# Two-block sequence kernel, fp32 on one core: reordering the second block's projections and the level steps of its gated linear attention

## The reference, cut to what matters

```
n = rms_norm(x, attn_norm_g)
proj = n @ w_in          # g_qkv (q 512, k 512, v 1024), g_lr 16, g_out 1024,
                         # nq 1024, kc vc ks vs kw vw 256 each, ng 24
g_qkv = silu(causal_short_conv(g_qkv, gla_conv_w))      # 4 taps along the tokens
log_a = log_sigmoid(g_lr @ gate_w2 + gate_b) / 16
# gated linear attention, chunks of 64 tokens, b = cumsum(log_a) in the chunk
scores = einsum('bhtd,bhsd,bhtsd->bhts', q, k, exp(b_t - b_s)), causal
o = scores @ v + (q * exp(b)) @ state;  state = decayed state + k^T v
gla_out = rms_norm(o) * silu(g_out)
nsa_out = compressed + selected + windowed attention over nq, kc, vc, ks, vs, kw, vw
h = x + concat([gla_out, nsa_out]) @ w_out
h + (silu(m @ w_gate) * (m @ w_up)) @ w_down            # m = rms_norm(h)
```

## Time and profile before

| | |
|---|---|
| median of 3 runs | 2771.13 us (2763.72 to 2773.09) |
| the profiled execution, its own time | 2766.11 us |
| its span, first to last instruction | 2764.1 us |
| granted TensorE clock, mean | 0.994 |
| TensorE busy | 2696.9 us, 98% of the span |
| VectorE, ScalarE, GpSimd busy | 1135.6, 1229.2, 1183.0 us (41%, 44%, 43%) |
| DMA | 489.00 MB, mean 177 GB/s |

### The profile page before, as it was taken

One profiled execution on the slowest core, in us unless ns is written; L12 is line 12 of the kernel. 1 busy time (PEld: TensorE's weight loads), 2 busy tenths in 40 slices (PEclk: granted clock), 3 DMA queues, 4 the chain that ended last, 5 costly groups with the idle time before them and its releaser, 6 DMA issues.

```text
span 2764.1 us, 33945 instructions
## 1 busy us (share of the span) xinstructions
PE 2696.9 (98%) x13886; PEld 2298.6 (83%) x13886; DVE 1135.6 (41%) x1363; ACT 1229.2 (44%) x1502; POOL 1183.0 (43%) x536
## 2 busy tenths in 40 slices
PE   9999999999999999999999978999999999999999
PEld 8998777778888888888888877988788888888887
DVE  6777654433432222232323477346432222232222
ACT  6434445444444444444444445535454444444333
POOL 3555553344444444444444334332244444444443
PEclk9999999999999999999999989999999999999999
DMA  6444445355555555555555532453355555555554
GB/s 235 163 158 155 156 139 174 137 198 187 193 183 189 192 186 195 185 192 191 196 192 198 180 129 101 170 189 124 132 184 185 193 187 191 190 188 193 197 199 152
DMA packets 73161, 489.00 MB, mean 177 GB/s; under 512 B 8443, under 2 KB 10140, under 8 KB 15536
## 3 DMA queue, kind: packets, MB, share of 16 engines
q1 hardware_dynamic: 73008, 486.84, 50.3%
HBM read 484.71 MB, written 2.10 MB: 176 GB/s over the span
## 4 chain that ended last, share of the span: by engine, by line
PE 85%; DVE 8%; ACT 3%; issue 3%; POOL 1%; DMA 1%; SPq 0%; DVEq 0%; ACTq 0%; POOLq 0%
PE PB L575 24%; PE PB L579 24%; PE PB L576 24%; PE PB L543 2%; PE PB L547 2%; PE PB L544 2%; ACT WH L1108 2%; PE PB L593 1%; DVE TM L2344 1%; DVE WL L1631 1%; DMA RAW<-in_w_in_a 1%; DVE TM L2341 1%; DVE TM L1683 1%; DVE TM L1674 1%; DVE TM L1686 0%
## 5 line engine op out<-in xcount | busy, mean ns | idle before, releaser
L2434 POOL TENSOR_TENSOR WL<-RAW,WH 128x1024 fp32r<-128x1024 f32 x442 | 1077.5, 2438 | 1462.4 <-ACT WH L1108 1462.4
L1108 ACT ACTIVATE WH<-RAW 128x1024 fp32r<-128x1024 f32 x892 | 939.6, 1058 | 1162.4 <-PE PB L579 1101.5
L1631 DVE TENSOR_TENSOR WL<-RAW,WH 128x1024 fp32r<-128x1024 f32 x450 | 581.8, 1294 | 1474.7 <-ACT WH L1108 1474.4
L575 PE MATMUL PB<-WH,HNH 128*128 128x512 f32 x1888 | 740.6, 392 | 5.0 <-DVE MIX L2279 4.6
L579 PE MATMUL PB<-WL,HNH 128*128 128x512 f32 x1888 | 735.5, 390 | 4.2 <-POOL WL L2434 4.2
L576 PE MATMUL PB<-WH,HNL 128*128 128x512 f32 x1888 | 735.1, 389 | 0.0
L575 PEld LDWEIGHTS PB<-WH,HNH 128*128 128x128 f32 x1888 | 354.6, 188 | 82.2 <-DVE MIX L2279 5.8
L579 PEld LDWEIGHTS PB<-WL,HNH 128*128 128x128 f32 x1888 | 354.6, 188 | 78.6 <-POOL WL L2434 4.6
L576 PEld LDWEIGHTS PB<-WH,HNL 128*128 128x128 f32 x1888 | 354.7, 188 | 72.1
L543 PE MATMUL PB<-HNH,WH 128*128 128x256 f32 x1184 | 347.1, 293 | 2.6 <-ACT WH L1108 2.4
L547 PE MATMUL PB<-HNH,WL 128*128 128x256 f32 x1184 | 339.4, 287 | 10.4 <-POOL WL L2434 6.0
(11 more groups left out here) (346 smaller groups left out, 2080.9 us busy)
## 6 DMA issues: line engine op xcount, KB each, us to landing
RAW<-in_w_gu SPq DMA_DIRECT2D x176, 1024.0 KB, 4.8
RAW<-in_w_dn SPq DMA_DIRECT2D x88, 1024.0 KB, 4.8
RAW<-in_w_in_a SPq DMA_DIRECT2D x56, 1024.0 KB, 4.8
RAW<-in_w_in SPq DMA_DIRECT2D x45, 1024.0 KB, 4.8
RAW<-in_w_out SPq DMA_DIRECT2D x32, 1024.0 KB, 4.8
RAW<-in_w_ga SPq DMA_DIRECT2D x24, 1024.0 KB, 4.8
RAW<-in_w_gb SPq DMA_DIRECT2D x24, 1024.0 KB, 4.8
WIN<-in_win SPq DMA_DIRECT2D x8, 512.0 KB, 5.8
```

Of the source, the lines that this page charges most:

```text
L575: e.matmul(o, hi[:, k, x], WH[:, s, c], start=k == 0, stop=False)
L1108: e.activation(WH[:, u % NSPL, :], RAW[:, n % NRAW, half * SU * 128:(half + 1) * SU * 128], ACT.Copy).then_inc(*wt.act.mark(("wh", u)))
L1631: e.tensor_tensor(WL[:, u % NSPL, :], RAW[:, n % NRAW, half * SU * 128:(half + 1) * SU * 128], f32(WH[:, u % NSPL, :]), ALU.subtract).then ...
L2434: e.tensor_tensor(WL[:, u % NSPL, :], RAW[:, n % NRAW, half * SU * 128:(half + 1) * SU * 128], f32(WH[:, u % NSPL, :]), ALU.subtract).then ...
```

## The change

- **Order of the projections.** `SECOND` becomes `og`, `ks`, `kc`, `v`, `vs`, `cmp`, `nq`, `mg`, and the weights are packed in that order. The number of tiles is the same.
- **Levels.** They run beside `og` and the first rows of `ks`. A fourth buffer of exponents is added (`GE3`, in memory that the queries `NQA` use later). VectorE's `before(lv)` and GpSimd's `after(lv)` stand in step 3 + lv, ScalarE's exponential in step 4 + lv, `keys(lv)` and `queries(lv)` in step 5 + lv, TensorE's matmuls in step 6 + lv, `taken(lv)` in step 7 + lv.
- **Convolutions.** VectorE now scales row j and does not convolve it there: `conv_next(j)` runs the three last taps of row j - 1 (`conv4`) and then scales row j. The first tap moves to ScalarE (`conv_first`, an activation with a scale, in the place of the `tensor_scalar`). The silus move one row back. The turning of `v` moves one tile back (tile 9 of the row).
- **Outputs.** The output part of the linear attention (`outputs`) starts eight quick steps into `vs` and ends in `cmp`; the norms of the keys and `CB` (`keys`) come ahead of it, beside `kc` and the first row of `v`. `CB` and a small norm buffer (`NB2`) move in memory.

The core of the diff (the moved helper functions of the other attention are unchanged and left out):

```diff
-        GE = [ar("GE0", [128, 4, T], 32), ar("GE1", [128, 4, T], 36), GG]
+        GE = [ar("GE0", [128, 4, T], 32), ar("GE1", [128, 4, T], 36), GG, ar("GE3", [128, 4, T], 76)]
...
-        CB = ar("CB", [128, 2, 32, 2, 15], 16)
+        CB = ar("CB", [128, 2, 32, 2, 15], 32)
...
-        SECOND = (("v", 8, 16), ("og", 2, 64), ("ks", 4, 16), ("kc", 4, 16), ("vs", 1, 64),
+        SECOND = (("og", 2, 64), ("ks", 4, 16), ("kc", 4, 16), ("v", 8, 16), ("vs", 1, 64),
...
+        def second(w, levels, keys, outputs, heads):
+
+            yield from levels
+            w.rate = 3.4 / 16.0
             yield from passed(w, "ks", 3)
-            for _ in range(4):
-                yield
+            yield from keys
+            w.passed.add("cb")
+            yield from passed(w, "v", 7)
+            yield from idle(8)
+            yield from outputs
+            yield from passed(w, "cmp", 1)
+            yield from heads
+
+        def other_levels():
+            return idle(14)
+
+        def other_keys(w):
+            yield from idle(4)
...
+        def other_outputs():
+            return idle(10)
...
-                        group(nt, HNH, HNL, 16)
+                        group(nt, HNH, HNL, 16, None, {1: values_turned})
                     elif name == "og":
-                        group(NT["og"] + 2 * j, HNH, HNL, 16, None, {} if j else {1: values_turned, 2: gates_turned})
+                        group(NT["og"] + 2 * j, HNH, HNL, 16, None, {} if j else {2: gates_turned})
...
+            def conv_first(j):
+
+                e.wait_ge(*m.dve.done("cs4", j))
+                if 2 <= j < 10:
+                    e.wait_ge(*m.act.done("c", j - 2))
+                if j >= 10:
+                    e.wait_ge(*m.pe.done("v", j - 10))
+                e.activation(TM[:, (2 * j + 1) % 4, :], TM[:, 2 * j % 4, :], ACT.Copy, scale=vec("gw3", j)).then_inc(
+                    *m.act.mark(("c4", j)))
+
+            taps = {(2, 12): (0,), (3, 3): (1,), (3, 11): (2,), **{(j + 1, 2): (j,) for j in range(3, 8)}}
+            silus = {(3, 5): (0,), (3, 13): (1,), (4, 4): (2,), **{(j + 2, 4): (j,) for j in range(3, 7)}, (8, 12): (7,)}
+
...
-                    if j > 3 and k == 1:
-                        conv_silu(j - 1)
-                if j == 2:
-                    for p in range(3):
+                    for p in taps.get((j, k), ()):
+                        conv_first(p)
+                    for p in silus.get((j, k), ()):
                         conv_silu(p)
...
+            def value_silu(j):
+                e.wait_ge(*m.dve.done("c", 8 + j))
+                x = TM[:, (2 * j + 1) % 4, :]
+                e.activation(x, x, ACT.Silu).then_inc(*m.act.mark(("v", j)))
...
+                        if k == 2 and (name == "v" and j or name == "vs"):
+                            conv_first(8 + (j - 1) % 8)
+                        if k == 4 and (name == "v" and j > 1 or name == "vs"):
+                            value_silu((j - 2) % 8)
+                        if k == 10 and name == "vs":
+                            value_silu(7)
...
+                for lv in range(11):
+                    if lv < 8:
+                        before(lv)
+                    if 2 <= lv < 10:
+                        keys(lv - 2)
+                    if 4 <= lv:
+                        taken(lv - 4)
+                    yield
...
-            def conv4(nt, j, freed):
+            def conv4(j):
+
                 s, y = TM[:, 2 * j % 4, :], TM[:, (2 * j + 1) % 4, :]
-                scaled(nt, s, freed)
-                e.wait_ge(*m.dve.prev())
-                if 2 <= j < 10:
-                    e.wait_ge(*m.act.done("c", j - 2))
-                if j >= 10:
-                    e.wait_ge(*m.pe.done("v", j - 10))
-                e.tensor_scalar(y, s, vec("gw3", j), None, ALU.mult).then_inc(*m.dve.mark())
+                e.wait_ge(*m.act.done("c4", j))
                 for i in range(1, 4):
-                    e.wait_ge(*m.dve.prev())
+                    if i > 1:
+                        e.wait_ge(*m.dve.prev())
                     e.scalar_tensor_tensor(out=y[:, i:T], in0=s[:, 0:T - i], scalar=vec(f"gw{3 - i}", j),
                                            in1=y[:, i:T], op0=ALU.mult, op1=ALU.add).then_inc(
                                                *m.dve.mark(*([("c", j)] if i == 3 else [])))
 
+            def conv_next(first, j):
+
+                if j % 8:
+                    conv4(j - 1)
+                nt = first + j % 8
+                scaled(nt, TM[:, 2 * j % 4, :], [("cs4", j), ("free", nt)])
+
+            scalings = {(2, 9): (0,), (2, 16): (1,), (3, 9): (2,), **{(j, 16): (j,) for j in range(3, 8)}}
             e.wait_ge(landed["lmask"], 16)
             e.tensor_copy(LM[:, :, :], LM4[:, :, :]).then_inc(*m.dve.mark("lm"))
...
+                for lv in range(10):
+                    if lv < 8:
+                        after(lv)
+                    if lv >= 2:
+                        queries(lv - 2)
+                    yield```

Three places in the instruction order show what moved. Buffer numbers stand behind the names.

**ScalarE in the levels.** Before, from the first exponential beside `v` on (L1595 is a silu of `v`, L1242 an exponential of a level):

```order
L1242 ACTIVATE GE0_117<-GE0_117 128x1024
L1108 ACTIVATE WH_50<-RAW_49 128x1024 x2
L1595 ACT_TABLE_LOAD
L1595 ACTIVATE TM_57<-TM_57 128x256
L1242 ACT_TABLE_LOAD
L1242 ACTIVATE GE1_118<-GE1_118 128x1024
L1108 ACTIVATE WH_50<-RAW_49 128x1024
L1242 ACTIVATE GG_115<-GG_115 128x1024
L1108 ACTIVATE WH_50<-RAW_49 128x1024
L1595 ACT_TABLE_LOAD
```

306 lines of the change are left out of this document (129 added, 177 removed).

## The result

| | before | changed |
|---|---|---|
| median of 5 runs, us | 2773.09 (2763.72 to 2774.88) | 2752.83 (2751.39 to 2753.02) |
| profiled execution: own time, span | 2766.11, 2764.1 | 2751.39, 2749.4 |
| ratio of times | | 0.9935, 95% interval 0.9921 to 0.9948 |

The changed kernel is faster by 0.65%; by the interval it saves 14 to 22 us. The two profiled spans differ by 14.7 us, the medians by 20.3.

The account below looks back on a forecast made before the run. TensorE's waits and low clock in the second block were taken as the bound. Terms 0 + 4.2 + 14.6 - 2 - 2.3 - 1.5 = 13.0 us gained, so 2771.1 - 13.0 = 2758.1 us, range 2746 to 2773.

Parts of the forecast that it names:

- What bounds: Whole kernel: a gain can only come from TensorE's waits and its low clock in the second block.
- Rows of `c`: Stretch up to the gate's matmul: late rows stay late at 7.1 us each; 0, between 6.6 us gained and 1 lost.
- Rival A: In the rows of `c`: they run on time, so later parts start 6.6 us earlier, total 2751.5 us; chance 0.15.
- Gate to first level: From gate matmul to first level: level starts at the same time, TensorE has done 12.3 tiles more; 4.2 us gained.
- Levels: First to last level: of 17.6 us lost before, 3 stay lost, at 5.97 us a TensorE step; 14.6 us gained.
- Rival B: In the levels: VectorE and GpSimd stay the bound, 8.4 us a step, total 2772 us, no change; chance 0.14.
- Table loads: On ScalarE: six fewer loads, at 1.28 us each without the skill's extra 1.38 us drain, gain nothing.
- Rows of `v`: Second block: `CB` additions delay the first turned `v`, then rows keep TensorE's 5.98 us, margin 0.35 us; 2 us lost.
- rival C: Third tap of each `v` row: falls behind GpSimd's half, seven rows lose 25 us, total 2783 us; chance 0.11.
- Outputs: In `cmp`: the first heads are ready late, so TensorE waits 1.9 and 0.3 us; 2.3 us lost.
- Smaller waits: Last turning of `v` in `vs` 0.2 us, the rest low clock behind waits; 1.5 us lost.
- From span to median: Whole kernel: 2753 us against the profiled execution, plus the 5 us by which the old median lay above it: 2758.1 us.

## Why the prediction was right, and where it was off

- **What bounds.** Right: what went is idle time and time at the lower clock in the second block. Of the 17.6 us lost in the old levels 10.9 were waits; the clock (0.90 over 63 us) accounts for most of the rest.
- **Rows of `c`: 0, measured -2.1.** The mechanism held: late rows stay late at 7.16 us (forecast 7.06), held taps, gate at 1619.1 (1618.3). The new convolution cost 0.8, inside the bound of 1; the other 1.3 is the clock behind `X`, which the sum did not have. The wait of 3.9 us at the gate came as 1.2 there and as four waits of about half a microsecond in the halves of `og` ahead of it; with `v` behind `lr` it is one wait of 3.6, and the gate's matmul stands at the same place. Rival A fell as a forecast, and giving the halves to VectorE brought it about: the gate at 1613.3.
- **Gate to first level: 4.2, measured 4.8.** The size was right and the place wrong. I put a wait of 4 to 5 us at the first level. It had none; TensorE waited 1.8 and 2.6 us for low halves, 1.0 for the silu of `og` and 1.2 at the second level. I had followed one chain, VectorE's and GpSimd's work ahead of the level, and not asked what else stands in the queues that this chain holds up.
- **Levels: 14.6, measured 14.9.** 6.0 to 6.1 us apart but for two steps (7.3 and 6.8). Rival B (8.4 a step) did not come: the mask copies out of PSUM are not held up, and the exclusive work fits. But my reading of why was half of it. I counted the step of its own as the cause and put no price on the convolutions beside the levels. Old steps in the new order and new steps in the old order both come out at the old time or above; the gain needs both.
- **Table loads: 0.** Right; the load ahead of `og`'s silu takes 1.28 us, begins 0.02 us behind the end of the exponential ahead of it, and the silu starts 0.02 behind the load.

```profile
1648.75 1.28 ACT L1618 ACT_TABLE_LOAD   x1
1650.05 1.27 ACT L1618 ACTIVATE OG<-PB,RTOK 128x512 f32<-128x512 f32 x2
```

The Trainium skill (ScalarE: Activation LUTs, What ACT_TABLE_LOAD costs) adds a drain of 1.38 us to the load; this trace has none on either side of it.

- **Rows of `v`: -2, measured about -1.** One wait of 0.8 us at the first turned `v`, then the pace of 6.0; no turn of GpSimd's half ahead of VectorE's. The margin is 0.57 us in most rows (forecast 0.35), and the tripled copies showed its price: 14 us, where rival C said up to 25.
- **Outputs: -2.3, measured -1.8 (waits of 1.6 and 0.2).** Right. Its worth to the median was not: taking the wait away gave nothing measurable.
- **Smaller waits: -1.5.** Too dear up to `HIDT`: the last three terms made 5.8 and 2.5 were lost. Behind it nothing was forecast and 1.6 us were lost, of which 1.4 is the clock: the kernel with the old convolution of `c` has the same waits there, one of 1.1 us for the squares of the queries among them, and is only 0.2 us longer than before.
- **From span to median.** This is the step that missed by most. The sum of 13.0 stands against 13.5 in the traces from `X` on, or 14.7 with the difference ahead of `X`. That this is so close is partly luck: the last three parts were 3.3 us too dear, and the clock, which was in no part, took 2.7. I then carried over the 5 us by which the old median lay above its profiled execution. The changed kernel's median lies 1.4 us above its own. Both traces of the kernel before come from the lower end of its times (2766.1 of 2764 to 2778), so where the others spend 5 to 10 us more is open. Their mean granted clock is on record, though: of the 57 runs beside the experiments the ten under 2767 us have 0.992 to 0.994, the nine above 2777 us 0.987 or 0.988. So the longer runs are those with more time at the lower clock; behind which waits isn't recorded. The kernel with old steps in the new order, with the most waits behind one another of the new-order kernels, spreads as widely (2764.6 to 2777.2).

## What to carry to other kernels

Giving each part of a pipelined job a step of its own paid here only where every engine's work fitted into the step; count what the engines exclude each other on, and move unrelated work away first (here neither change alone showed anything). A helper engine that makes half of a load in 2.4 us and blocks the other engine meanwhile can cost more than the 1.2 us it saves: look for operations that end just behind the helper's. Before a difference of 1 or 2 us between two traces is put down to an edit, compare the granted clock behind the same waits. And make a sum against a profiled span stay one: the gap between one execution and a median belongs to that kernel and not to the next.
